# Cycling a group's experts in descending order, and moving an early expert block's products, weighing and transposes among the routing products of a one-core decoder step

## The chip, the cores and the metric

The kernel runs on one core of a Trainium2 chip. The metric is the device time in microseconds (us) of one execution; less is better. Three runs of the kernel before took 1231.51, 1237.66 and 1239.29 us.

## What is computed

One layer of a decoder: stick-breaking attention beside a convolution module, an output projection, and then a mixture of experts (MoE) over 1,056 tokens (1,024 of a prompt, 32 of samples). The change touches only the MoE and its routing. Cut to that:

```
logits = tokens @ w_router                         # 16 experts in 4 groups of 4
probs  = softmax(logits); sel = probs + b_router
best   = group with the largest sum of its two largest sel
idx    = the 2 experts with the largest sel in that group
w      = probs[idx] / sum(probs[idx])
y      = sum over the 2 experts of  w * (silu(t @ w_gate[e]) * (t @ w_up[e])) @ w_down[e]
x_out  = x + gate * y
```

Everything is float32. `w_gate[e]` and `w_up[e]` are 1024 x 512, `w_down[e]` is 512 x 1024: 2 MB each, 6 MB an expert. On the inputs that setup_inputs draws, the reference's router sends this many of the 2,112 (token, expert) pairs to experts 0 to 15: 43, 57, 52, 90 | 104, 184, 147, 39 | 116, 69, 65, 48 | 348, 115, 175, 460. Of the first 512 tokens, expert 15 has 224, more than any other.

## The kernel before, in words

**The early expert.** While the output projection and the router still run over the last token tiles, the expert with most of the first 512 tokens (here 15) is chosen, its three weights are loaded into side 0 of the weight buffers, and up to 256 of its tokens are worked on in NEB = 2 blocks of 128 rows, s = 0 and 1. A block's work is: TensorE transposes its rows (`early_turn`), `early_gate_or_up(s, 0, ...)` is the gate product and `early_gate_or_up(s, 1, ...)` the up product over k = 0 to 7 (KD = 8; one k is one 128x128 by 128x512 float32 product, two records of the trace); ScalarE takes the sigmoid, VectorE multiplies (`early_swish`, L2603) and then weighs with the up product and the router weight (`early_weigh`, L2607); TensorE transposes the result (`early_turn_act`, L1895), ScalarE copies it out of PSUM (`evac_acte`, L1335), and TensorE multiplies by w_down (`early_down(s, w)`, two halves w). VectorE ends a block with `early_combine` (L2613), and GpSimd scatters it.

**The routing.** TensorE transposes the normed rows of tile t (`route`, L1831), multiplies them with the router's weights (`router_strips`, L1842) and adds the strips (`router_sum`, L1849). With the last `router_sum` VectorE starts a long chain of small operations: the choice of experts, the mask `r_maskb` (L2693), then a wait for `rank_ready`, which TensorE gives after the rank products (L1964 to L1968), then slots, units and the ordering (L2706 to L2792). At L2790 it releases TensorE's first `to_slots` (L1978), which gives the token rows of the first passes; VectorE turns them into indices (L2797 to L2800) and GpSimd fetches those rows of x (`fetch_x`, L971). VectorE goes on with `tile_w` (L2809), the expert lists (`experts_of`, L2761 to L2777), the two `early_combine`, the copies to `w_slot` and `turned_hi(0)` (L2834). The gate product of pass 0 (L2007) waits for `turned_hi(0)`, the two combines and its weights. All of TensorE's and VectorE's order is written out by hand; each engine runs its instructions in program order.

**Units and passes.** An expert's remaining tokens are cut into units of UR = 64 rows. Units stand in one list, expert after expert. Pass t works on two units at once, unit t on side 0 and unit r_cut + t on side 1, with r_cut = max(half the units, the units of the largest group); each side has one buffer for each of the three weights. The expert order starts at the early expert, takes its group first and the other groups in a cycle, and inside each group cycles from the early expert's member number on. `expert_order` (L2585 on) computes it from `e_parts`: part 0 is each expert's group, part 1 its number in the group.

**The loop.** `step(t)` on TensorE: up product of pass t, the transposes of pass t + 1 in its middle (L1998), gate product of pass t + 1 with the transposes of the activations (L2014), down product of pass t (L2021). On SP, `refill(t)` loads w_up of pass t + 1 when the up product of pass t is done, w_gate of pass t + 2 when the gate product of t + 1 is done, and w_down of pass t + 1 when the down product of t is done, all by L782. A load is conditional: it moves nothing when the side keeps its expert. SP first waits, before the weights of pass 0 (L779 to L792), for all four gate and up products of the early blocks. GpSimd gathers x rows, residual rows and gate rows and scatters the result each pass.

Of the kernel before, what the change touches and what calls it, by code (L numbers as in the profile page):

```python
# [8 lines left out]
ALU = mybir.AluOpType  # L9
# [29 lines left out]
def decoder_step(nc, x_prompt, x_sample, cache_k, cache_v, state_conv, page_table, c_prompt, c_sample,  # L39
# [12 lines left out]
    CW, CC = conv_w.shape[1:]  # L52
    TAIL = CW - 1
    E, _, F = w_gate.shape[1:]
    EG = 4
    EPG = E // EG
    KD = D // P
# [44 lines left out]
    with ctx:  # L102
        def sb(name, shape, dt=F32):
            return ctx.enter_context(nc.sbuf_tensor(name, shape, dt))
# [68 lines left out]
        e_parts_i = sb("e_parts_i", [P, 2, E], I32)  # L173
        e_parts = sb("e_parts", [P, 2, E])
# [124 lines left out]
        def early(*shape, dt=F32):  # L299
# [10 lines left out]
            if len(shape) == 3:  # L310
# [81 lines left out]
                   "lgT_ps": ("c_sig", 1), "lgT_sb": ("rows_done", 2), "w_in_read": ("pool_const", 2),  # L392
                   "own_staged": ("ada_used", 32)}
        S |= {n: S[m] for n, (m, _) in (routing | merging).items()}

        MM_ALL = NCHUNK * NTP + 1
# [652 lines left out]
        def _(act):  # L1049
# [281 lines left out]
            def early_sigmoid(s):  # L1331
                act.wait_ge(S["e_gu"], N0["e_gu"] + s + 1)
                nc.scalar.activation(acte[:, s, :], bank[:, EG_BANK[s], :], ACT.Sigmoid).then_inc(S["e_sig"], 1)

            def evac_acte(s):  # L1335
                act.wait_ge(S["e_aps"], N0["e_aps"] + s + 1)
                nc.scalar.activation(acteT[:, s, :, :], bank[:, EA_BANK[s], :].rearrange("p (k n) -> p k n", k=KF), ACT.Copy)\
                    .then_inc(S["e_asb"], 1)
# [39 lines left out]
            nc.scalar.activation(r_e, r_z, ACT.Exp).then_inc(S["exp_ready"], 1)  # L1378
            for s in range(NEB):
                early_sigmoid(s)  # L1380
            act.wait_ge(S["hot_ready"], N0["hot_ready"] + 1)
            nc.scalar.activation(at_row32, at_row, ACT.Copy).then_inc(S["row32_ready"], 1)
            evac_acte(0)
            act.wait_ge(S["eq_ready"], 1)
            nc.scalar.activation(tile_id[:, :, 0, :], tile_id[:, :, 2, :], ACT.Copy, scale=part[:, 0:1])\
                .then_inc(S["part_ready"], 1)
# [44 lines left out]
        def _(pe):  # L1431
# [394 lines left out]
            def route(t):  # L1826
                pe.wait_ge(S["h2_done"], N0["h2_done"] + t + 1)
                if t >= 1:
                    pe.wait_ge(S["h2T_sb"], 2 * t)
                for k in range(KD if t < NTP else 2):  # L1830
                    mm = pe.transpose(bank[:, 4 + k // 4, (k % 4) * P:(k % 4 + 1) * P], h2[t % 2][:, k * P:(k + 1) * P],  # L1831
                                      identf[:, :])
                mm.then_inc(S["h2_ps"], 1)

            def router_strips(t):
                pe.wait_ge(S["h2T_sb"], 2 * t + 2)
                for i in range(KD // 4):
                    for j in range(4):
                        k = KD // 4 * j + i
                        n, turned = (P, h2T[:, t % 2, k, :]) if t < NTP else \  # L1840
                            (NS, h2T[:, t % 2, k % 2, NS * (k // 2):NS * (k // 2 + 1)])
                        mm = pe.matmul(lg_strip[NS * j:NS * j + E, t % 2, 0:n], wr[:, k, :], turned,  # L1842
                                       start=(i == 0), stop=(i == KD // 4 - 1))
                mm.then_inc(S["lgT_ps"], 1)

            def router_sum(t):
                n = P if t < NTP else NS
                pe.wait_ge(S["lgT_sb"], N0["lgT_sb"] + t + 1)
                pe.matmul(bank[0:n, 6, t * E:(t + 1) * E], lgT[:, t % 2, 0:n], strip_sum[:, 0:E], start=True, stop=True)\  # L1849
                    .then_inc(S["lg_mm"], 1)  # L1850
# [31 lines left out]
            def early_gate_or_up(s, w, k0, k1):  # L1882
                if w == 0 and k0 == 0:
                    pe.wait_ge(S["e_xsb"], N0["e_xsb"] + 2 * s + 2)
                if w == 1 and s == 1 and k0 == 0:
                    pe.wait_ge(S["h2T_sb"], 2 * NT)
                if k0 == 0:
                    pe.wait_ge(e_w_in[w], E_W0 + 16)
                for k in range(k0, k1):
                    mm = pe.matmul(bank[:, (EG_BANK, EU_BANK)[w][s], :], xeT[:, s, k, :], (wg_sb, wu_sb)[w][:, 0, k, :],  # L1890
                                   start=(k == 0), stop=(k == KD - 1))
                if k1 == KD:
                    mm.then_inc(S["e_gu"], 1)

            def early_turn_act(s):  # L1895
                pe.wait_ge(S["e_act"], N0["e_act"] + NEB + s + 1)
                for k in range(KF):
                    mm = pe.transpose(bank[:, EA_BANK[s], k * P:(k + 1) * P], acte[:, s, k * P:(k + 1) * P], identf[:, :])
                mm.then_inc(S["e_aps"], 1)

            def early_down(s, w):
                pe.wait_ge(S["e_asb"], N0["e_asb"] + s + 1)
                pe.wait_ge(e_w_in[2], E_W0 + 16)
                for k in range(KF):
                    mm = pe.matmul(bank[:, EY_BANK[s] + w, :], acteT[:, s, k, :], wd_sb[:, 0, k, w * 512:(w + 1) * 512],
                                   start=(k == 0), stop=(k == KF - 1))
                mm.then_inc(S["e_y"], 1)
# [42 lines left out]
            route(NTP - 1)  # L1950
            router_sum(NTP - 2)
            early_gate_or_up(0, 0, KD // 2, KD)
            route(NTP)
            router_strips(NTP - 1)
            early_gate_or_up(1, 0, 0, 2)
            router_sum(NTP - 1)
            router_strips(NTP)
            early_gate_or_up(1, 0, 2, 4)
            router_sum(NTP)
            early_gate_or_up(1, 0, 4, KD)  # L1960
            early_gate_or_up(0, 1, 0, KD // 2)
            pe.wait_ge(S["mask_ready"], N0["mask_ready"] + 2)
            ranks = bank[:, 0, 0:(NT + 1) * E]
            pe.matmul(ranks, identb[:, :], shift_used.rearrange("p t e -> p (t e)"), start=True, stop=False)  # L1964
# [9 lines left out]
            def to_slots(out, rows, cols, split):  # L1974
                for a in range(2 * NT):
                    n = cols(a).shape[-1]
                    for half, c0, c1 in ((slice(0, UR), 0, split), (slice(UR, P), split, n)):
                        mm = pe.matmul(out[half, :, 0:c1 - c0], rows[:, a, :], cols(a)[:, :, c0:c1],  # L1978
                                       start=(a == 0), stop=(a == 2 * NT - 1))
                mm.then_inc(S["slots_done"], 1)  # L1980

            early_gate_or_up(0, 1, KD // 2, KD)
            early_gate_or_up(1, 1, 0, 6)
            pe.wait_ge(S["hot_ready"], N0["hot_ready"] + 1)
            to_slots(bank[:, 1, 0:2 * NG].rearrange("p (w n) -> p w n", w=2), at_row,
                     lambda a: first_id[:, a, 0:2, :], NG)
            early_turn_act(0)
            early_gate_or_up(1, 1, 6, KD)
            early_down(0, 0)
            early_turn_act(1)  # L1990
            early_down(0, 1)
            pe.wait_ge(S["tok_ready"], 1)
# [123 lines left out]
        def _(dve):  # L2116
            c = Chain(dve, S["dve_c"])
            V = nc.vector
# [309 lines left out]
            c.put(V.tensor_scalar(e_parts_i[:, 0, :], row_no_i[:, 0:E], EPG.bit_length() - 1, None, ALU.arith_shift_right))  # L2428
            c.put(V.tensor_scalar(e_parts_i[:, 1, :], row_no_i[:, 0:E], EPG - 1, None, ALU.bitwise_and))
            c.wait()  # L2430
            c.put(V.tensor_copy(e_parts[:, :, :], e_parts_i[:, :, :]))
            c.put(V.tensor_copy(part[:, :], part_i[:, :]))
            c.put(V.memset(r_maskb, 0.0))
            c.put(V.memset(off_row[:, :], 0.0))
# [168 lines left out]
            def early_swish(s):  # L2603
                dve.wait_ge(S["e_sig"], N0["e_sig"] + s + 1)
                V.tensor_tensor(acte[:, s, :], acte[:, s, :], bank[:, EG_BANK[s], :], ALU.mult).then_inc(S["e_act"], 1)

            def early_weigh(s):  # L2607
                dve.wait_ge(S["e_gu"], N0["e_gu"] + NEB + s + 1)
                dve.wait_ge(S["e_act"], N0["e_act"] + NEB)
                V.scalar_tensor_tensor(acte[:, s, :], bank[:, EU_BANK[s], :], ew_slot[:, s:s + 1], acte[:, s, :],  # L2610
                                       ALU.mult, ALU.mult).then_inc(S["e_act"], 1)
# [86 lines left out]
                               AX_X, ALU.add))  # L2698
            for j in range(NEB):
                early_swish(j)  # L2700
            dve.wait_ge(S["rank_ready"], N0["rank_ready"] + 1)

            total = bank[:, 0, NT * E:(NT + 1) * E]
# [76 lines left out]
            def by_token(cols, n):  # L2780

                return cols.unsqueeze(1).broadcast_to([P, 2 * NT, n]), r_unit.unsqueeze(2).broadcast_to([P, 2 * NT, n])
# [7 lines left out]
                               ALU.is_equal))  # L2790
            dve.sem_inc(S["hot_ready"], 1)
            V.tensor_tensor(tile_id[:, :, 2, :], *by_token(unit_no, NC), ALU.is_equal).then_inc(S["eq_ready"], 1)  # L2792
            early_weigh(0)

            dve.wait_ge(S["slots_done"], N0["slots_done"] + 1)
            first = bank[:, 1, 0:2 * NG].rearrange("p (w n) -> p w n", w=2)
# [11 lines left out]
            dve.wait_ge(h2_stored[1], 16 * 4)  # L2808
            op(V.tensor_tensor(tile_w, tile_id[:, :, 2, :], r_w.unsqueeze(2).broadcast_to([P, 2 * NT, NC]), ALU.mult))  # L2809
            dve.sem_inc(S["hot_ready"], 1)  # L2810
            early_weigh(1)
            c.put(V.tensor_scalar(r_gm, units, -1.0, None, ALU.add))
            c.put(V.tensor_scalar(r_half, r_cut, -1.0, None, ALU.add))
            c.wait()
# [148 lines left out]
```

## Time and profile before

| | us |
|---|---|
| three runs | 1231.51, 1237.66, 1239.29; median 1237.66 |
| the profiled execution, its own time | 1229.6 |
| its span (first to last instruction) | 1227.9 |
| TensorE busy | 1152.1 |
| VectorE busy | 618.8 |
| mean granted TensorE clock | 0.987 of full |

Times of the trace are counted from the start of the span. The routing lies at about 740 to 790 us, the 18 passes of the MoE at 790 to 1220 us.

### The profile page before, as it was taken

Reading aid. Unit: us, or ns where it says so; the run is one execution under the profiler, and the core shown is the slowest. Engines: PE = TensorE matmul, PEld = TensorE weight load, DVE = VectorE, ACT = ScalarE, POOL = GpSimd, SP = SyncE. Lnnn points to the kernel's source line nnn. Section 1 sums busy time; section 2 is a strip of 40 time slices with the busy share of each in tenths; the row PEclk is TensorE's granted clock in tenths of the full one; section 3 lists DMA queues with packets and bytes.
Section 4 is the critical chain, followed back from the end, with each engine's and each line's share of the span. In section 5 each row is a group of like instructions: output and inputs, shape, how many; then the busy total and the mean of one; then the engine's idle time right before and its main releaser. Section 6 shows DMA issues by size and latency. Waiting matters only on the chain.

```text
span 1227.9 us, 19158 instructions
## 1 busy us (share of the span) xinstructions
PE 1152.1 (94%) x6692; PEld 541.4 (44%) x6692; DVE 618.8 (50%) x1254; ACT 341.2 (28%) x719; POOL 248.1 (20%) x303
## 2 busy tenths in 40 slices
PE   6999999999989889998999998989999999889995
PEld 4444444444436566665544453433333333333332
DVE  0010867786779999997974476611112121112112
ACT  2132221222137888887312321100000000000000
POOL 2011101221049600000010010112223222222222
PEclk9999999999999999999999999999999999999998
DMA  9943333322347454645332273779984668988983
GB/s 358 335 145 103 103 103 108 94 91 86 90 153 256 147 192 163 230 141 189 139 109 97 86 261 126 270 287 331 348 310 168 231 214 322 377 306 300 333 324 138
DMA packets 114100, 250.76 MB, mean 204 GB/s; under 512 B 14446, under 2 KB 28910, under 8 KB 113000
## 3 DMA queue, kind: packets, MB, share of 16 engines
q1 hardware_dynamic: 93345, 206.85, 48.0%
q0 software_dynamic: 16704, 38.30, 8.8%
q10 hardware_dynamic: 3984, 4.72, 1.1%
q8 instruction: 42, 0.69, 0.2%
q14 instruction: 25, 0.20, 0.1%
HBM read 370.93 MB, written 38.17 MB: 333 GB/s over the span
## 4 chain that ended last, share of the span: by engine, by line
PE 72%; DMA 10%; DVE 6%; issue 5%; ACT 4%; SPq 1%; POOL 0%; ACTq 0%; POOLq 0%; DVEq 0%
PE bank L1598 20%; PE bank L2007 15%; PE bank L2021 7%; PE bank L1789 6%; DMA low<-out_dram,o_col 3%; PE bank L1578 3%; PE bank L1632 2%; PE bank L1672 2%; DMA out_dram<-mid,o_col 2%; PE bank L1682 2%; DMA big<-in_w_up_dram 2%; PE bank L1660 2%; PE bank L1453 1%; ACT mid L1231 1%; PE bank L1695 1%
## 5 line engine op out<-in xcount | busy, mean ns | idle before, releaser
L2007 PE MATMUL bank<-big,mid 128*64 128x512 f32 x1120 | 255.0, 602 | 13.0 <-DMA big<-in_w_gate_dram 7.2
L1598 PE MATMUL bank<-big 128*128 128x512 f32 x560 | 249.2, 598 | 0.1
L1598 PEld LDWEIGHTS bank<-big 128*128 128x128 f32 x560 | 103.6, 190 | 131.3 <-issue 131.3
L2182 DVE SCALAR_TENSOR_TENSOR cvT<-low,cw,cvT 128x256 f32<-128x256 f32 x360 | 156.9, 514 | 0.0
L2007 PEld LDWEIGHTS bank<-big,mid 128*64 128x64 f32 x1120 | 79.4, 138 | 161.0 <-issue 160.2
L2021 PE MATMUL bank<-big,mid 128*64 128x512 f32 x544 | 119.6, 592 | 0.0
L2287 DVE TENSOR_TENSOR_SCAN big<-big 128x513 f32<-128x513 f32 (+4 forms) x96 | 90.3, 980 | 8.4 <-ACT big L1198 8.4
L2897 DVE TENSOR_TENSOR mid<-bank,low 128x512 f32<-128x512 f32 x34 | 21.9, 686 | 126.8 <-DMA low<-out_dram,o_col 81.0
L2878 DVE TENSOR_TENSOR xt<-xt,bank 128x512 f32<-128x512 f32 x18 | 12.4, 687 | 140.4 <-ACT xt L1395 140.4
L889 POOL TENSOR_TENSOR st<-st,mhalf 128x16 f32<-128x16 f32 (+1 forms) x9 | 25.2, 2801 | 254.3 <-DVE st L2213 245.5
L2021 PEld LDWEIGHTS bank<-big,mid 128*64 128x64 f32 x544 | 39.1, 137 | 77.7 <-issue 77.7
L1390 ACT ACTIVATE mid<-bank 128x512 f32<-128x512 f32 x18 | 10.8, 598 | 190.2 <-PE bank L1998 190.2
L1789 PE MATMUL bank<-mid,cvT 128*128 128x512 f32 x128 | 58.2, 602 | 1.1 <-DVE cvT L2390 1.1
L1789 PE MATMUL bank<-mid,big 128*128 128x512 f32 x128 | 58.1, 596 | 0.0
L1198 ACT ACTIVATE big<-bank,nbb 128x512 f32<-128x512 f32 (+3 forms) x96 | 50.9, 586 | 17.3 <-PE bank L1638 11.9
L1660 PE MATMUL bank<-identf,big 128*128 128x128 f32 x288 | 45.8, 286 | 9.4 <-ACT big L1221 3.3
L2297 DVE TENSOR_TENSOR big<-big 128x512 f32<-128x512 f32 (+3 forms) x96 | 53.3, 592 | 0.4
L1211 ACT ACTIVATE big<-bank,bb 128x512 f32<-128x512 f32 (+3 forms) x96 | 51.3, 601 | 0.0
L1003 POOL DMA_INDIRECT out_dram<-mid,o_col x17 | 17.1, 1004 | 167.5 <-DVE mid L2899 167.5
L2338 DVE SCALAR_TENSOR_TENSOR cvT<-low,cw,cvT 128x256 f32<-128x256 f32 x120 | 50.8, 489 | 0.0
L1083 ACT ACTIVATE big<-bank,low 128x128 f32<-128x128 f32 x64 | 23.4, 468 | 90.7 <-PE bank L1492 58.5
L1632 PE MATMUL bank<-big 64*128 64x512 f32 (+3 forms) x192 | 44.9, 545 | 3.2 <-ACT big L1211 2.0
(460 smaller groups left out, 1386.9 us busy)
## 6 DMA issues: line engine op xcount, KB each, us to landing
big<-in_w_gate_dram SPq DMA_DIRECT2D x39, 2048.0 KB, 9.3
big<-in_w_up_dram SPq DMA_DIRECT2D x37, 2048.0 KB, 8.3
big<-in_w_down_dram SPq DMA_DIRECT2D x37, 2048.0 KB, 13.6
low<-in_w_ada_dram SPq DMA_DIRECT2D x32, 512.0 KB, 4.1
low<-in_cache_v_dram SPq DMA_DIRECT2D x64, 256.0 KB
big<-in_w_in_dram SPq DMA_DIRECT2D x8, 1280.0 KB, 17.1
xt<-in_x_prompt_dram SPq DMA_DIRECT2D x16, 512.0 KB, 4.7
mid<-in_w_ada_dram SPq DMA_DIRECT2D x8, 1024.0 KB, 14.0
```

The source lines that it names most:

```text
L1198: nc.scalar.activation(keep[w][h][:, first:first + n], bank[:, 2 * (i % 2) + h, 0:n], ACT.Sigmoid, scale=-(HD ** -0.5), bias=nbb[:, 2 * pa ...
L1211: nc.scalar.activation(sig[w][h][:, b0 * P:b1 * P], bank[:, 2 * (i % 2) + h, 0:n], ACT.Sigmoid, scale=HD ** -0.5, bias=bb[:, 2 * pair + h: ...
L1598: mm = pe.matmul(bank[:, 4 if cc == 2 else cc, :], hT[:, s, k, :], w_in_sb[:, k, cc * 512:(cc + 1) * 512], start=(k == 0), stop=(k == KD - 1))
L1632: mm = pe.matmul(bank[:, 2 * (i % 2) + h, 0:n], stage[64 * h:64 * h + 64, s, 0, qb * P:(qb + 1) * P], stage[64 * h:64 * h + 64, s, 1, b0 * ...
L1660: mm = pe.transpose(bank[:, TURN_BANK["a", 2 * i + h], (kb - b0) * P:(kb - b0 + 1) * P], sig[u % 2][h][:, kb * P:(kb + 1) * P], identf[:, :])
L1789: mm = pe.matmul(bank[:, 2 * (t % 2) + cc, :], cat[:, k % NPAIR, t * P:(t + 1) * P], w_out_sb[:, k, cc * 512:(cc + 1) * 512], start=(k == ...
L2007: mm = pe.matmul(bank[half, 2 * s + w, :], xgT[:, s, k, half], w_sb[:, x, k, :], start=(k == 0), stop=(k == KD - 1))
L2021: mm = pe.matmul(bank[half, 6 + w, :], actT[:, s, k, half], wd_sb[:, x, k, w * 512:(w + 1) * 512], start=(k == 0), stop=(k == KF - 1))
L2182: c.put(V.scalar_tensor_tensor(out, src, cw[:, ch, tap:tap + 1], out, ALU.mult, ALU.add))
L2287: V.tensor_tensor_scan(kept, kept, kept, 1.0, ALU.mult, ALU.bypass).then_inc(S["scan_done"], 1)
L2297: V.tensor_tensor(sig[w][h][:, b0 * P:b1 * P], sig[w][h][:, b0 * P:b1 * P], keep[w][h][:, first + b0 * P:first + b1 * P], ALU.mult).then_i ...
L2338: c.put(V.scalar_tensor_tensor(out, x, cw[:, ch, tap:tap + 1], out, ALU.mult, ALU.add))
```

## The change

It does three things: (a) part 1 of `e_parts` becomes 3 minus the member number, so that inside each group the cycle runs downwards (15, 14, 13, 12 and not 15, 12, 13, 14), with one more small VectorE operation for it; (b) on TensorE, pieces of the early blocks' products move among the routing products, and the first transpose of the activations and a down product move ahead of the first `to_slots`; (c) on ScalarE and VectorE, `evac_acte(0)` and both `early_weigh` move to earlier places.

```diff
@@ ScalarE
             for s in range(NEB):
                 early_sigmoid(s)
+            evac_acte(0)
             act.wait_ge(S["hot_ready"], N0["hot_ready"] + 1)
             nc.scalar.activation(at_row32, at_row, ACT.Copy).then_inc(S["row32_ready"], 1)
-            evac_acte(0)
@@ TensorE
             early_gate_or_up(0, 0, KD // 2, KD)
+            early_gate_or_up(1, 0, 0, 3)
             route(NTP)
             router_strips(NTP - 1)
-            early_gate_or_up(1, 0, 0, 2)
+            early_gate_or_up(1, 0, 3, 4)
             router_sum(NTP - 1)
             router_strips(NTP)
-            early_gate_or_up(1, 0, 2, 4)
+            early_gate_or_up(1, 0, 4, 5)
             router_sum(NTP)
-            early_gate_or_up(1, 0, 4, KD)
-            early_gate_or_up(0, 1, 0, KD // 2)
+            early_gate_or_up(1, 0, 5, KD)
+            early_gate_or_up(0, 1, 0, KD)
             pe.wait_ge(S["mask_ready"], N0["mask_ready"] + 2)
@@ TensorE
-            early_gate_or_up(0, 1, KD // 2, KD)
             early_gate_or_up(1, 1, 0, 6)
+            early_turn_act(0)
+            early_gate_or_up(1, 1, 6, KD)
+            early_down(0, 0)
             pe.wait_ge(S["hot_ready"], N0["hot_ready"] + 1)
             to_slots(bank[:, 1, 0:2 * NG].rearrange("p (w n) -> p w n", w=2), at_row,
                      lambda a: first_id[:, a, 0:2, :], NG)
-            early_turn_act(0)
-            early_gate_or_up(1, 1, 6, KD)
-            early_down(0, 0)
             early_turn_act(1)
@@ VectorE
-            c.put(V.tensor_copy(e_parts[:, :, :], e_parts_i[:, :, :]))
+            c.put(V.tensor_copy(e_parts[:, 0, :], e_parts_i[:, 0, :]))
+            c.put(V.tensor_scalar(e_parts[:, 1, :], e_parts_i[:, 1, :], -1.0, EPG - 1.0, ALU.mult, ALU.add))
@@ VectorE
             for j in range(NEB):
                 early_swish(j)
+            early_weigh(0)
             dve.wait_ge(S["rank_ready"], N0["rank_ready"] + 1)
@@ VectorE
             V.tensor_tensor(tile_id[:, :, 2, :], *by_token(unit_no, NC), ALU.is_equal).then_inc(S["eq_ready"], 1)
-            early_weigh(0)
+            early_weigh(1)
 
             dve.wait_ge(S["slots_done"], N0["slots_done"] + 1)
@@ VectorE
             dve.sem_inc(S["hot_ready"], 1)
-            early_weigh(1)
```

## Rows read from the trace of the kernel before

**Rows 1.** The page's chain that ended last, by engine.

```profile
PE 72%; DMA 10%; DVE 6%; issue 5%; ACT 4%; SPq 1%; POOL 0%; ACTq 0%; POOLq 0%; DVEq 0%
```

**Rows 2.** Timeline of PE, 736 to 801 us: start, us, engine, line, shapes, [idle before].

```profile
736.44 3.68 PE L1890 MATMUL bank<-big 128*128 128x512 f32 x8
742.18 0.44 PE L1831 MATMUL bank<-identf,low 128*128 128x128 f32 x2 [2.06 <-DVE low L2476]
...
747.30 0.24 PE L1849 MATMUL bank<-strip_sum,big 128*32 128x16 f32 x2
...
756.30 0.24 PE L1964 MATMUL bank<-big,identb 128*128 128x160 bf16 x1 [1.70 <-DVE r_maskb L2693]
...
765.59 0.73 PE L1978 MATMUL bank<-first_id,low 128*64 128x4 bf16 x36
767.71 0.69 PE L1898 MATMUL bank<-identf,xt 128*128 128x128 f32 x4 [1.38 <-DVE xt L2610]
768.20 3.58 PE L1890 MATMUL bank<-big 128*128 128x512 f32 x4
...
786.75 2.94 PE L1978 MATMUL bank<-low 128*64 128x40 f32 x108
790.33 10.52 PE L2007 MATMUL bank<-big,mid 128*64 128x512 f32 x48 [0.64 <-issue]
```

**Rows 3.** Timeline of DVE, 757 to 791 us.

```profile
757.14 1.29 DVE L2605 TENSOR_TENSOR xt<-xt,bank 128x512 f32<-128x512 f32 x2
758.34 0.43 DVE L2706 TENSOR_TENSOR mid<-bank,ramp 128x272 f32<-128x272 f32 x1
...
766.90 0.75 DVE L2610 SCALAR_TENSOR_TENSOR xt<-bank,ew_slot,xt 128x512 f32<-128x512 f32 x1
767.57 0.15 DVE L2797 COPY mid<-bank 128x2 f32<-128x2 f32 x1
...
772.48 0.14 DVE L2812 TENSOR_SCALAR mid<-mid 128x1 f32<-128x1 f32 x1
...
782.14 1.29 DVE L2619 TENSOR_TENSOR cvT<-bank,low 128x512 f32<-128x512 f32 x2 [0.26 <-DVE pass_exp L2777]
...
789.54 0.69 DVE L2834 COPY mid<-bank 128x512 f32<-128x512 f32 x1
```

**Rows 4.** Timeline of PE in the loop, 809 to 1111 us.

```profile
809.30 5.26 PE L2007 MATMUL bank<-big,mid 128*64 128x512 f32 x16 [3.84 <-DMA big<-in_w_gate_dram]
...
879.94 3.65 PE L2007 MATMUL bank<-big,mid 128*64 128x512 f32 x16 [1.28 <-DVE mid L2834]
...
1055.93 1.09 PE L1998 MATMUL bank<-identf,mid 128*128 128x128 f32 x8
1063.98 5.35 PE L2007 MATMUL bank<-big,mid 128*64 128x512 f32 x16 [3.37 <-DMA big<-in_w_gate_dram]
...
1084.26 3.65 PE L2007 MATMUL bank<-big,mid 128*64 128x512 f32 x16 [3.89 <-DMA big<-in_w_up_dram]
1087.85 1.09 PE L1998 MATMUL bank<-identf,mid 128*128 128x128 f32 x8
...
1110.36 1.10 PE L1998 MATMUL bank<-identf,mid 128*128 128x128 f32 x8
```

**Rows 5.** Timeline of SP: when the weight loads of L782 were issued (two sides each).

```profile
797.83 0.83 SPq L782 DMA_DIRECT2D big<-in_w_gate_dram  x2
...
1046.11 1.10 SPq L782 DMA_DIRECT2D big<-in_w_gate_dram  x2
...
1061.21 4.50 SPq L782 DMA_DIRECT2D big<-in_w_up_dram  x2
```

**Rows 6.** Windows: length, busy us of PE, PEld, DVE, ACT, POOL; PEclk, DMA share, GB/s.

```profile
809.30:815.00 5.70, 5.70 (x20) 1.96 (x20) 0.00 (x0) 0.00 (x0) 0.00 (x0) 0.71 1.03 396
...
1061.00:1084.30 23.30, 16.43 (x70) 5.61 (x71) 3.85 (x5) 1.19 (x2) 4.72 (x7) 0.93 1.02 383
```

**Rows 7.** DMA issues after 800 us, median us from issue to landing.

```profile
mid<-h_d,x_col POOLq DMA_INDIRECT x18, 7.7
```

## The prediction

> **What bounds the kernel now.** I read the chain that ended last first: TensorE holds 72% of it and DMA 10% [rows 1], so a change pays where TensorE stands idle or at half clock. Next came TensorE's timeline over the two stretches that the change touches. In the routing it idles 2.06 us before the last `route`, 1.70 before the rank products and 1.38 before the transpose of block 0, and the four records after that take 3.58 us where eight took 3.68 before [rows 2]: two k at the lower of its two clock levels, some 1.7 us lost. After that it is busy to pass 0, which starts at 790.33, just after VectorE's `turned_hi(0)` of 789.54 + 0.69 [rows 2, 3]. In the loop the trace shows a pass each 22.51 us (1087.85 to 1110.36) except where weights come late: the gate product of pass 1 waits 3.84 us, a `turned_hi` behind a late gather holds that of pass 4 for 1.28 us, and from pass 11 to pass 12 the transposes stand 31.92 us apart, 9.41 over the usual 22.51 [rows 4]. That is 3.37 for w_gate, 3.89 for w_up and half clock after the first: 5.35 us for sixteen records that take 3.65 otherwise.
>
> **Part 1, the order.** Expert 15 keeps 460 - 224 = 236 pairs, 4 units. With units of 64 the experts 0 to 15 have 1, 1, 1, 2 | 2, 3, 3, 1 | 2, 2, 2, 1 | 6, 2, 3, 4 units, 36 in all; the largest group has 15, so r_cut = 18 and there are 18 passes, in both kernels. Before, side 0 runs 15 (4 units), 12 (6), 13 (2), 14 (3), 3 (2), 0 (1), and side 1 runs 1, 2, 7 (1 each), 4 (2), 5 (3), 6 (3), 11 (1), 8, 9, 10 (2 each). A new expert is due at passes 4, 10, 12, 15, 17 on side 0 and 1, 2, 3, 5, 8, 11, 12, 14, 16 on side 1. The only pass with both is 12, and it follows 10 and 11: just where the 9.41 us are [rows 4]. After, side 0 is 15 (4), 14 (3), 13 (2), 12 (6), 3 (2), 2 (1), due at 4, 7, 9, 15, 17; side 1 is 1, 0, 7 (1 each), 6 (3), 5 (3), 4 (2), 11 (1), 10, 9, 8 (2 each), due at 1, 2, 3, 6, 9, 11, 12, 14, 16. Fourteen loads of 6 MB both times. Again one pass has both, now 9, but pass 8 has none, nor has 10.
>
> So the double is not removed; it gets an empty queue. Its w_gate was issued at 1046.11, w_up at 1061.21 [rows 5], and at full share DMA moves 396 GB/s, 383 over the whole stretch with w_up [rows 6]; I take 0.40 MB a us. A double weight is 4.19 MB. The gathers and the scatter are four of 0.52 MB a pass. Let G be the issue of the double w_gate of pass 9. Its product was due at G + 14.5 before (1063.98 - 3.37 = 1060.61 against 1046.11). The w_gate load of pass 1, issued at 797.83 and in at 809.2, took 11.4 us for 2.1 MB and about three gathers, 3.67 / 0.40 = 9.2 us, so I put 2 us ahead of the first byte. With these and 4.19 / 0.40 = 10.5 us it lands at G + 12.5; the x gather of the pass has gone before it, since with light DMA the chain of gathers runs ahead. No wait. (If 1 MB of gathers falls in, G + 15: 0.5 us.) The double w_up is issued at G + 15.1 and starts at G + 17; with three gathers beside it, 5.75 MB / 0.40 = 14.4 us, it lands at G + 31.3. It is due after gate and down products, 14.5 us behind G + 14.5 or G + 29.1. Wait: 2.2 us. The double w_down has 16 us and 6.3 MB: just in time. Before, w_up had the rest of w_gate and w_down of pass 11 ahead, hence its wait and the full share of 1.02. So the double costs 2.1 us rather than 9.41: **-7.3 us**. Bounds: nothing (-9.4) and both waits kept at some two thirds of their size with one half-clock stretch (-3). Passes 1 to 4 load as before and keep the 1.28; pass 5 is now free, worth 0.2 us that I set against the extra `e_parts` operation, on a VectorE with slack.
>
> **Part 2, the routing stage.** One k costs 3.68 / 8 x 2 = 0.92 us with its tail, 0.88 by the pitch [rows 2].
> - Three k fill the idle before the last `route`: they end at 740.0 + 2.65 = 742.65, so `route` starts 0.47 late, but two k fewer (-1.76) stand between it and the last `router_sum`, which moves from 747.30 to 746.0: VectorE's whole choice of experts runs 1.3 us earlier, the mask is ready at 755.0.
> - TensorE then has 3 + 8 k = 9.7 us, to 755.95, so ranks start there (before 756.30) without idling, and are out at 756.6. VectorE's swishes end 1.3 earlier, about 757.1; `early_weigh(0)` adds 0.67 in front of L2706, which starts at 757.75 and not 758.34. Ranks hide behind the weighing. Gain on VectorE's chain 0.6 us.
> - TensorE: six k, the transpose (0.5), two k, a down product (3.45) end at 767.5. The first `to_slots` is released at 764.9 and now waits behind these: 767.5 to 768.2, where it ran at 765.59. What is queued behind that on others: L2797 (767.57) starts at 768.35, 0.8 later, and with it the x fetch. VectorE loses the 0.8 but no longer stops 1.3 us for the second weighing, so L2812 comes at 771.3 for 772.48, `early_combine(0)` at 780.9 for 782.14.
> - TensorE, without gaps and without the 1.7 us of half clock, ends the last down product at 779.05. The second combine used to wait for it; now it follows the first directly, 780.9 + 2 x 2.56 = 786.0. Then `w_slot` 0.44 and `turned_hi` 0.69: pass 0 can start at 787.3 for 790.33. **-3.0 us.** VectorE is the bound now; TensorE has finished its 1.0 of transposes and 2.94 of slots by 783.0 and idles 4.3 us.
>
> That idle has a price. Idle stretches of 3.84 and 3.37 us were followed by 5.26 and 5.35 us for sixteen records, that of 3.89 by 3.65 [rows 4], the granted clock after the first being 0.71 [rows 6]. So between 0 and 1.7 us are lost in the gate product of pass 0; two of three, and the one behind slot products with few columns, say yes: **+1.65**. The Trainium skill, TensorE: Matmul & The Clock Gate, the section on HAM oscillation, says that waits between bursts of products put the clock back to its lower level so that each burst begins slow. By that rule the loss is full here; the row of 3.89 shows that it isn't certain.
>
> **Part 3, what follows at pass 1.** SP waits for the four early products; the last ends at 764.05, before 771.8. So the 6 MB of pass 0 start 7 us earlier and are through by 782, and DMA is empty when the blocks are scattered; the gathers of pass 0 start some 3 us earlier against the gate load of pass 1. That load was issued at 797.83 and arrived 11 us later, DMA at full share [rows 5, 6]; its product is due 8.06 us after issue plus 0.4. If gathers of 0.5 to 1 MB have left before, it comes 1.3 to 2.6 us sooner, and half clock in pass 0 stretches nothing else. I take 0.9 us left of 3.84, **-2.9 us**, and with so short a stop no half clock after it (the 1.28 us stop had none [rows 4]), **-1.6 us**. Bounds: wait and clock loss kept (0), both gone (-5.5).
>
> Sum: -7.3 - 3.0 + 1.65 - 2.9 - 1.6 = -13.1 us. The profiled execution of 1229.6 would be 1216.5. It lies 8.1 us under the median of the runs; I subtract the same from the median: 1237.7 - 13.1 = 1224.6 us.
>
> **Rivals.**
> - A: the x fetch is late. It is issued 0.8 us later and now comes after, not before, the 6.3 MB of weights. Its landing was 7.7 us in the median [rows 7], for it to matter it must need over 12.8 (TensorE needs it by 782). If it waited for the weights, 766.6 + 16 = 782.6, and its own 1.05 MB gives 785.2, then 1.0 + 2.94 + 1.1: pass 0 at 790.3, nothing gained there. Only -7.3 and perhaps -1: 1230 us. For: DMA share 1.03 in such stretches. Against: gathers in the loop land in 7.7 beside weights. The Trainium skill, DMA: Bandwidth & Descriptors, section on queues, rings and completion order, says that each DMA engine takes turns among the queues that have work, a packet at a time; by that rule the fetch gets its share and this rival falls.
> - B: the double keeps its price, because what made it dear is its 12.6 MB alone and not what stood ahead. Then only parts 2 and 3 remain, -5.8: 1232 us. For: three double weights in a row still use all of DMA. Against: the fluid sum above. The same time comes out if the direction did not move the double at all.
> - C, slower: at pass 9 all three double weights are late, not two, each by what the rows show (3.84, 3.37, 3.89) with half clock after each (1.65): 16.1 us for 9.41, so +6.7, and the start's gain of 5.8 doesn't cover it: +0.9, 1238.6 us. It decides when w_down's 6.3 MB take over 16 us, below 0.39 MB a us; 383 GB/s over a stretch is under that, but a late w_up also moves w_down's due time, which speaks against it.
>
> **How the numbers follow.** The forecast 0.54, A 0.19, B 0.20, C 0.07. A measurement of this kernel can tell about 1% (12.4 us) from nothing. The forecast's own spread (bounds of part 1 -9.4 to -3, of parts 2 and 3 -9 to -1) puts it beyond 1% in nearly nine tenths, as timed runs sit above the profiled one and so seem to wait more than it: 0.48. The rest and A and B are within 1% but for few: 0.46. C past 1% or trouble unseen: 0.06. Range: -20 to -1 around 1237.7, 1217 to 1236.
>
> **What would show it.** Right: no 31.9 us pass at pass 12; the passes around 9 together 2 us long, waiting for w_up; the last `router_sum` at 746.0; L2706 at 757.75; first slots at 767.5; pass 0 at 787.3 behind `turned_hi`, with about 4 us idle before it and a clock under 1; the wait for pass 1's w_gate near 1 us. Wrong: a wait for the x rows before L1998 at 779, waits for weights at pass 9 summing to over 6 us, or VectorE standing before `early_weigh(0)`.

## The result, and the profile after

Ten runs of the changed kernel have a median of 1226.86 us (1224.46 to 1230.49), ten of the kernel before beside them 1238.01 us (1231.51 to 1244.97): a ratio of 0.9919 with a 95% interval of 0.9896 to 0.9942, 0.8% faster. The forecast was 1224.6 us with a range of 1217 to 1236. The profiled execution of the changed kernel took 1228.0 us, only 1.6 us less than that of the kernel before (1229.6): the first is near its median, the second lies under all ten runs of its kernel. So the two traces are compared stretch by stretch here, and what a stretch costs in general is read from the fourteen traces of this study.

The page of the changed kernel, span and chain, against [rows 1]:

```profile
span 1226.2 us, 19159 instructions
...
PE 76%; DMA 8%; DVE 6%; ACT 5%; issue 4%; SPq 0%; ACTq 0%; POOL 0%; POOLq 0%; DVEq 0%
```

DMA gave up 2 points of the chain, and TensorE's share is 4 points up. TensorE's timeline of the changed kernel over the routing, against [rows 2]:

```profile
738.94 6.25 PE L1890 MATMUL bank<-big 128*128 128x512 f32 x14
745.03 0.38 PE L1831 MATMUL bank<-identf,low 128*128 128x128 f32 x2
...
748.38 0.24 PE L1849 MATMUL bank<-strip_sum,big 128*32 128x16 f32 x2
...
758.09 0.23 PE L1965 MATMUL bank<-big,identb 128*128 128x160 bf16 x1
...
769.53 0.73 PE L1979 MATMUL bank<-first_id,low 128*64 128x4 bf16 x36
...
781.96 2.94 PE L1979 MATMUL bank<-low 128*64 128x40 f32 x108
789.23 13.19 PE L2007 MATMUL bank<-big,mid 128*64 128x512 f32 x48 [4.33 <-DVE mid L2835]
```

From the last common product to 784.90, the end of the slot products, TensorE runs without a gap now; the three idle stretches of 2.06, 1.70 and 1.38 us are gone. In their place stands one of 4.33 us before pass 0, and it waits for VectorE. The 48 records behind it take 13.19 us where they took 10.52. VectorE, against [rows 3]:

```profile
759.63 0.75 DVE L2611 SCALAR_TENSOR_TENSOR xt<-bank,ew_slot,xt 128x512 f32<-128x512 f32 x1
760.30 0.43 DVE L2708 TENSOR_TENSOR mid<-bank,ramp 128x272 f32<-128x272 f32 x1
...
770.31 0.16 DVE L2799 COPY mid<-bank 128x2 f32<-128x2 f32 x1 [0.70 <-PE bank L1979]
...
783.07 1.29 DVE L2620 TENSOR_TENSOR cvT<-bank,low 128x512 f32<-128x512 f32 x2 [0.26 <-DVE pass_exp L2779]
784.40 1.23 DVE L2622 TENSOR_TENSOR cvT<-cvT,low 128x1024 f32<-128x1024 f32 x1
785.54 1.28 DVE L2620 TENSOR_TENSOR cvT<-bank,low 128x512 f32<-128x512 f32 x2
...
788.43 0.69 DVE L2835 COPY mid<-bank 128x512 f32<-128x512 f32 x1
```

The second combine follows the first with no gap, and `turned_hi(0)` ends at 789.12, 0.1 us before pass 0. The clock there, in windows of the changed kernel (columns as in [rows 6]):

```profile
789.00:796.00 7.00, 6.78 (x20) 2.41 (x22) 2.73 (x18) 0.00 (x0) 2.55 (x4) 0.60 0.32 127
796.00:802.00 6.00, 6.00 (x30) 2.02 (x26) 0.69 (x1) 0.60 (x1) 2.71 (x4) 1.00 0.60 174
```

The loop, against [rows 4]:

```profile
812.42 4.97 PE L2007 MATMUL bank<-big,mid 128*64 128x512 f32 x16 [5.39 <-DMA big<-in_w_gate_dram]
...
989.48 1.09 PE L1998 MATMUL bank<-identf,mid 128*128 128x128 f32 x8
997.23 3.65 PE L2007 MATMUL bank<-big,mid 128*64 128x512 f32 x16 [3.07 <-DMA big<-in_w_gate_dram]
...
1014.16 3.65 PE L2007 MATMUL bank<-big,mid 128*64 128x512 f32 x16 [2.24 <-DMA big<-in_w_up_dram]
1017.75 1.09 PE L1998 MATMUL bank<-identf,mid 128*128 128x128 f32 x8
```

Pass 12 is like any other; the double stands at pass 9 and costs 28.27 - 22.51 = 5.76 us over, for 9.41. But pass 1 waits 5.39 us for w_gate where it waited 3.84.

Where the first pair of traces hides the gain: TensorE's first long group of projection products.

```profile
22.34 15.69 PE L1578 MATMUL bank<-big 128*128 128x512 f32 x36 [2.16 <-ACT big L1083]
```

That was the kernel before; the changed one:

```profile
23.23 17.38 PE L1578 MATMUL bank<-big 128*128 128x512 f32 x36 [2.16 <-ACT big L1083]
```

No edit lies there, yet by the last common product before the routing the changed kernel's trace is 2.5 us late (738.94 for 736.44). At an L1731 product ahead of every edit the traces of this study stand between 573.6 and 577.9 us, 574.8 before and 577.3 after. Whether that is scatter between executions isn't shown: the second traces of the same two kernels stand at 574.6 and 577.5, each within 0.2 us of its first, so it may as well belong to the program as built. It is left out of the sums below, but a difference of a few us between two medians may come from there.

### The profile page after: what moved, and what is told of

Same layout as the page of the kernel before. It is cut to its first block, busy times and chain, and to the rows that moved or that the text cites. A ratio compares the mean times of both kernels' runs of the same rounds, so it can differ in the third digit from the quotient of the medians.

```text
span 1226.2 us, 19159 instructions
## 1 busy us (share of the span) xinstructions
PE 1152.6 (94%) x6692; PEld 541.3 (44%) x6692; DVE 619.2 (50%) x1255; ACT 340.8 (28%) x719; POOL 248.1 (20%) x303
## 4 chain that ended last, share of the span: by engine, by line
PE 76%; DMA 8%; DVE 6%; ACT 5%; issue 4%; SPq 0%; ACTq 0%; POOL 0%; POOLq 0%; DVEq 0%
PE bank L1598 20%; PE bank L2007 16%; PE bank L2021 7%; PE bank L1789 7%; PE bank L1578 3%; DMA low<-out_dram,o_col 3%; PE bank L1632 2%; PE bank L1890 2%; PE bank L1672 2%; PE bank L1682 2%; PE bank L1660 2%; DMA out_dram<-mid,o_col 2%; DMA big<-in_w_up_dram 2%; PE bank L1453 1%; ACT mid L1231 1%
```

## The experiments

Each kernel was timed beside the kernel before, and has one trace. The runs came in three groups, e1 to e4, e5 to e8 and e9 to e12, in which the kernel before had medians of 1236.26, 1239.52 and 1238.30 us; across groups the ratio to it is the better measure. "After" below is the changed kernel.

**The order alone (e1).** The kernel before with only the `e_parts` edit.

```diff
-            c.put(V.tensor_copy(e_parts[:, :, :], e_parts_i[:, :, :]))
+            c.put(V.tensor_copy(e_parts[:, 0, :], e_parts_i[:, 0, :]))
+            c.put(V.tensor_scalar(e_parts[:, 1, :], e_parts_i[:, 1, :], -1.0, EPG - 1.0, ALU.mult, ALU.add))
```

> Only the descending cycle, everything else as before. Theory 1 (the order makes most of the gain, by giving the double load of pass 9 an empty queue): 6 to 10 us under the kernel before in the median; in the trace the pass with both loads costs 5.8 us over 22.51 and stands at pass 9, not 9.4 at pass 12. Rival (the gain is from the routing stage): under 3 us in the median.

1227.05 us for 1236.26, ratio 0.9916 (0.9884 to 0.9948): nearly all of the gain. Its trace was taken in the slowest of its nine executions (1232.46 us). In it the passes 2 to 8 lie exactly 22.51 us apart and pass 9 costs 4.64 over, but pass 1 costs 9.20:

```profile
1001.94 5.10 PE L2007 MATMUL bank<-big,mid 128*64 128x512 f32 x16 [2.57 <-DMA big<-in_w_gate_dram]
1018.26 3.65 PE L2007 MATMUL bank<-big,mid 128*64 128x512 f32 x16 [0.19 <-DMA big<-in_w_up_dram]
```

All passes together are 13.9 us over, for 17.0 and 20.2 in the two traces of before, so the loop of this trace shows 3 to 6 of the 9.2 us. In the routing it even loses time: the last `router_sum` stands 12.58 us behind the last common product, for 10.86, since the idle of 2.20 us before the last `route` was followed by half clock (3.09 us for four records that take 1.98 otherwise). In e9, with the same old places, it was so again; in the two traces of before it wasn't.

**The places alone (e2).** After with the old `e_parts` line (the diff above reversed).

> Only the moved products, weighing and transposes, the order ascending as before. Theory 1: 1 to 4 us under the kernel before; pass 0 starts 3.5 us earlier against the last early product before the routing, but its sixteen first records run at half clock and the wait for w_gate of pass 1 stays at 4 to 5.5 us, so that little is left. Rival (the stage's 3.6 us are all kept and the double at pass 12 costs less, too): 5 us or more.

1234.73 us for 1236.26, ratio 0.9985 (0.9957 to 1.0014): nothing that can be told from no change. Pass 0 starts 40.81 us after the last `router_sum`, for 43.03 before, behind 4.31 us of idle; its 48 records take 12.01 us, and w_gate of pass 1 is waited for 7.18 us.

**Both again (e3, e4).** The two kernels unchanged, for second traces.

> The kernel before, unchanged, for a second trace. Its profiled execution was 8 us under the median of its runs. Theory 1 (typical executions wait longer for weights in the loop than the profiled one did): a trace near the median shows over 9.4 us at pass 12 and more than 1.7 us in the passes 3 to 5. Rival (the difference lies ahead of the routing, as the 2.5 us between the two traces at 736 us do): the loop as in the first trace and the last product before the routing later.

> The changed kernel, unchanged, for a second trace on this chip. Theory 1: 11 us under the kernel before in the median; idle of about 4.3 us before pass 0, a wait of 4 to 5.5 us for w_gate of pass 1, 5 to 6 us over at pass 9. Rival (the 5.39 us wait for w_gate of pass 1 was chance): 1 to 3 us there.

Before: 1235.72 us; pass 1 costs 8.75 over (5.67 in the first trace), pass 12 10.90. So its first profiled execution was a lucky one in the loop, by 3.2 us over all passes. The passes 3 to 5 cost 0.37 only, which my theory had above 1.7. After: 1225.72 us, ratio 0.9909 (0.9877 to 0.9940); idle 4.30, wait at pass 1 5.57, pass 9 3.90, under the 5 to 6 expected. The wait of 5.39 was no chance. Against e2, in the same group of runs, the order is worth 9.0 us by the medians, as it was alone (9.2).

**No pass with two loads (e5).** After, but only the early expert's group descends: `e_parts` is as before the change, and on `b_two`, after the wrap, a member part x over 0 becomes 4 - x where the group part is 0.

```diff
+                c.put(V.tensor_scalar(b_wrap[:, 0, :], b_two[:, 0, :], 0.0, None, ALU.is_le))
+                c.put(V.tensor_scalar(b_wrap[:, 1, :], b_two[:, 1, :], 0.0, None, ALU.is_gt))
...
+                op(V.tensor_tensor(b_two[:, 1, :], b_two[:, 1, :], b_wrap[:, 0, :], ALU.add))
```

> The changed kernel, but only the early expert's own group cycles downwards, the others upwards as before: side 0 takes a new expert at passes 4, 7, 9, 15, 17, side 1 at 1, 2, 3, 5, 8, 11, 12, 14, 16, so no pass has both. Theory 1 (what costs is a pass with both loads, by the queue): the 4 to 6 us over at pass 9 fall under 1, the median 3 to 5 us under the changed kernel. Rival (the loads at 7, 8 and 9 in a row cost the same): no change, waits over 3 us at passes 8 and 9.

1224.80 us, ratio 0.9885 (0.9853 to 0.9917), against 0.9919 and 0.9909 for after: the intervals overlap, and the 3 to 5 us that theory 1 has are not clear of noise. The passes 8 and 9 cost nothing now, as theory 1 says. But the ascending side 1 brings a load at pass 5 back, the fifth in a row, and there the trace has what I had priced at 0.2 us:

```profile
906.71 5.35 PE L2007 MATMUL bank<-big,mid 128*64 128x512 f32 x16 [3.50 <-issue]
```

3.50 us of waiting and half clock after it, 5.42 over for that pass, 0.42 for the one ahead. The wait is put down to nothing in this row, but VectorE shows its end:

```profile
903.27 1.29 DVE L2904 TENSOR_TENSOR mid<-bank,low 128x512 f32<-128x512 f32 x2 [13.60 <-DMA low<-out_dram,o_col]
...
905.73 0.68 DVE L2841 COPY mid<-bank 128x512 f32<-128x512 f32 x1
```

The combine stood waiting for its residual rows, `turned_hi` comes behind it in VectorE's order and ended at 906.41, and the product started 0.3 us later. So this pass was held by a late gather and not by a late weight.

**The gathers held back (e6).** After, with one wait on GpSimd.

```diff
+            pool.wait_ge(wg_in[1], 32)
             gather_out(0, 0, 1, 16)
```

> The changed kernel; GpSimd starts the gathers of output rows of pass 0 only when w_gate of pass 1 has landed. Theory 1 (the wait for w_gate of pass 1 comes from gathers that run beside it): it lands some 8 us after issue rather than 13, the wait falls from 5.5 to about 0 to 1 us, 4 to 7 us less in the median with the half clock gone. Rival (2 MB takes that long by itself at this place): the wait stays over 4 us and the median within 2 us.

1227.21 us, nothing won in the median, yet both halves of it are instructive:

```profile
808.16 3.65 PE L2008 MATMUL bank<-big,mid 128*64 128x512 f32 x16 [1.97 <-DMA big<-in_w_gate_dram]
...
882.31 4.97 PE L2008 MATMUL bank<-big,mid 128*64 128x512 f32 x16 [5.79 <-DVE mid L2836]
```

The wait at pass 1 falls to 1.97 us and the half clock behind it goes: the product starts 9.6 us after the issue of w_gate, not 13.0. The gathers held it up. Then the gathers themselves are late, and at pass 4 TensorE waits 5.79 us for a `turned_hi` that stands on VectorE behind a combine whose rows are late: 7.32 over for that pass. The gain was given back three passes later.

**The combines ahead of the long list (e7).** After, on VectorE.

```diff
-            experts_of(MT, pass_exp)
-            dve.sem_inc(S["tiles_ready"], 1)
             for j in range(NEB):
                 early_combine(j)
...
             turned_hi(0)
+            experts_of(MT, pass_exp)
+            dve.sem_inc(S["tiles_ready"], 1)
```

> The changed kernel; VectorE's long expert list for all passes comes after the two combines and turned_hi(0), not before. Theory 1 (VectorE's chain alone sets the start of pass 0): it starts 3 to 3.5 us earlier, TensorE idles about 1 us before it and keeps the full clock; 3 to 5 us less if the wait for w_gate of pass 1 doesn't grow. Rival (that wait takes it back, since the gathers and the load meet anyway): the start is earlier, the median within 1.5 us.

1218.00 us, ratio 0.9842 (0.9810 to 0.9875), 9 us under after, where theory 1 had 3 to 5. VectorE:

```profile
779.33 1.29 DVE L2620 TENSOR_TENSOR cvT<-bank,low 128x512 f32<-128x512 f32 x2
...
782.39 1.29 DVE L2620 TENSOR_TENSOR cvT<-bank,low 128x512 f32<-128x512 f32 x2 [0.51 <-PE bank L1905]
...
785.94 0.69 DVE L2833 COPY mid<-bank 128x512 f32<-128x512 f32 x1
```

and TensorE:

```profile
786.73 10.52 PE L2007 MATMUL bank<-big,mid 128*64 128x512 f32 x48 [0.64 <-issue]
...
804.90 3.65 PE L2007 MATMUL bank<-big,mid 128*64 128x512 f32 x16 [3.04 <-DMA big<-in_w_gate_dram]
```

VectorE waits for TensorE again. The span is 1215.2 us for 1226.2. Pass 0 starts 37.15 us after the last `router_sum` (which ran at 749.58), 3.7 earlier than in after, at full clock. The wait at pass 1 fell, too, to 3.04, for a reason that I had not put in the expectation. SP issued the load at 794.23, and GpSimd, which now gets its indices later, its gathers behind it (the next fence); in after those of L990 to L998 stood ahead of a load issued at 799.39, and only the x gathers behind (the one after that). The double at pass 9 fell as well, from 5.76 to 2.67 us; why isn't shown.

```profile
795.58 1.06 POOL L990 DMA_INDIRECT low<-out_dram,o_col  x1 [0.92 <-POOL o_col L984]
796.94 0.96 POOL L992 DMA_INDIRECT low<-g_d,o_col  x1 [0.30 <-issue]
803.40 1.00 POOL L998 DMA_INDIRECT low<-out_dram,o_col  x1 [5.50 <-DMA low<-out_dram,o_col]
```

```profile
795.56 0.96 POOL L992 DMA_INDIRECT low<-g_d,o_col  x1 [0.30 <-issue]
798.12 1.00 POOL L998 DMA_INDIRECT low<-out_dram,o_col  x1 [1.60 <-DMA low<-out_dram,o_col]
...
800.11 0.98 POOL L979 DMA_INDIRECT mid<-h_d,x_col  x1 [0.79 <-POOL x_col L976]
```

**Filler in the idle (e8).** After, with four products whose result nothing reads.

```diff
+            pe.wait_ge(S["e_done"], N0["e_done"] + 1)
+            for k in range(4):
+                pe.matmul(bank[:, 6, :], identf[:, :], cv_flat[:, 0:512], start=True, stop=True)
```

> The changed kernel with four products of 128x512 that nothing reads put into the idle before pass 0, 3.5 us of work. Theory 1 (the idle sets the clock back and that costs 1.5 to 2.7 us in pass 0): the first 48 records of the loop take 10.5 us rather than 12.2 to 13.2, the clock is full there, and the median falls by 1 to 2.5 us. Rival (the wait for w_gate of pass 1 swallows it, as its load is issued at the end of the gate product, or the clock falls for another reason): median within 1 us.

1226.51 us, no change; the rival holds, and the trace shows both sides:

```profile
784.42 3.70 PE L2040 MATMUL bank<-cvT,identf 128*128 128x512 f32 x8 [0.77 <-DVE cvT L2625]
788.05 10.52 PE L2007 MATMUL bank<-big,mid 128*64 128x512 f32 x48
...
810.47 6.08 PE L2007 MATMUL bank<-big,mid 128*64 128x512 f32 x16 [7.28 <-DMA big<-in_w_gate_dram]
```

The idle did set the clock back: filled, the 48 records take 10.52 us. But the wait for w_gate grows from 5.4 to 7.28. Counted from the last `router_sum`, its load goes out 2.6 us sooner, and it takes 14.8 us for 12.9.

**Combines first in three other settings (e9, e10, e11).** The e7 edit on e1, on e5, and on e2.

> Descending order and the combines ahead of the long expert list, but the products, weighing and transposes in their old places. Theory 1 (the moved products shorten TensorE's side, which the old place of the list hid): the second combine still waits for the last early down product at 785.9 of the first trace, so pass 0 starts within 1 us of before and the median lies within 2 us of the order alone (1227). Rival (the place of the list is worth 3 to 4 us by itself): 1222 to 1224.

1227.74 us, ratio 0.9904 (0.9873 to 0.9936): theory 1. Without the moved products pass 0 starts 43.02 us after the last `router_sum`, as before; the place of the list is worth nothing there, since the second combine waits for TensorE, 4.26 us here.

> The kernel with the combines first, with the mixed order that has no pass with two loads but five passes in a row with one and then three more. Theory 1 (a row of five loads without a pause loses what the double loses, through late gathers or weights): 0 to 5 us over near pass 4 or 5 instead of the 2.7 at pass 9, the median within 2 us of 1218. Rival (the loss there was chance): 2.5 to 4 us under it.

1214.55 us, ratio 0.9809 (0.9781 to 0.9836), the fastest kernel of the study and 3.5 us under e7 by the median: the number of the rival. The traces don't show it in the loop. All passes together are 5.70 us over here and 5.99 in e7, as 2.67 us saved at pass 9 stand against half clock at pass 1, where e7 had none, and 0.57 at pass 5. But this trace stands at 573.6 us at the L1731 product ahead of every edit and e7's at 577.9, and that is 4.3 of the 4.8 us between their spans. What the missing double is worth stays open. The row of five cost little this time, again behind VectorE's combine:

```profile
800.65 5.35 PE L2007 MATMUL bank<-big,mid 128*64 128x512 f32 x16 [3.16 <-DMA big<-in_w_gate_dram]
...
892.96 3.65 PE L2007 MATMUL bank<-big,mid 128*64 128x512 f32 x16 [0.34 <-issue]
```

> All moved places and the combines first, but the ascending order. Theory 1 (the order is worth 7 to 10 us in any setting): 1225 to 1229, with 8 to 11 us over at pass 12. Rival (the double was only dear because the loop began late at pass 1): under 1222.

1228.30 us, ratio 0.9919 (0.9890 to 0.9949), 10.3 above e7, from which it differs by the order alone: theory 1. Pass 12 costs 11.75 over, and the passes 4 and 5 1.48 and 6.81. At pass 5 TensorE waits 4.89 us, as in e5 behind a combine for whose residual rows VectorE stood idle:

```profile
894.59 1.29 DVE L2897 TENSOR_TENSOR mid<-bank,low 128x512 f32<-128x512 f32 x2 [14.98 <-DMA low<-out_dram,o_col]
```

Most of such an idle costs nothing: in e1, where TensorE doesn't wait at these passes, VectorE idles 9.47 and 6.54 us for its rows.

**x rows before output rows (e12).** e7, with one gather moved ahead on GpSimd.

```diff
+            pool.wait_ge(S["xg_ps"], 1)
+            gather_x(2, 0, 1)
             for s in range(NEB):
                 pool.wait_ge(out_st[s], EARLY)
-            gather_out(0, 0, 1, 16)
-            pool.wait_ge(S["xg_ps"], 1)
-            gather_x(2, 0, 2)
+            gather_out(0, 0, 2, 16)
```

> The kernel with the combines first; GpSimd fetches the x rows of pass 2 before it waits for the scatters of the early blocks, in a stretch where DMA stands idle. Theory 1 (each 0.5 MB of gathers that runs beside w_gate of pass 1 delays it by about 1.3 us): the wait there falls from 3.0 to 1 to 2 us and the median by 1 to 2 us, without the late gather at pass 4 that holding all of them back brought. Rival (no change, since other gathers close up): within 0.5 us.

1220.82 us, ratio 0.9855 (0.9828 to 0.9883), against e7's 1218.00, so if anything slower. The stretch was not idle for long: the gather was issued at 792.47, 1.3 us behind w_gate (791.21), and the wait at pass 1 was 4.50 us, not 1 to 2. The load took 1.4 us longer with this gather beside it than in e7, near the 1.3 that theory 1 has for 0.5 MB; the theory was wrong in where the gather would fall.

**The fourteen traces side by side** (us over the 22.51 of a pass, from one L1998 group to the next; "landing" is from the issue of w_gate of pass 1 on SP to the start of its product, less 0.1; "xb" is when the gather of L998 was issued against that load):

```
                       xb    landing  pass 1  passes 3-5  the double
before                +4.8   11.4      5.67      1.69      9.41
e3 before again       +3.7   14.0      8.75      0.37     10.90
e1 order              +3.9   15.0      9.20      0         4.64
e2 places             +0.3   14.7      8.94      0        10.46
after                 -1.3   12.9      6.93      0.10      5.76
e4 after again        -0.3   13.1      8.36      0         3.90
e5 no double          -0.7   13.0      8.00      5.84      none
e8 filler             +2.1   14.8      9.93      0         7.12
e12 x before out     +11.2   12.0      6.17      0         3.50
e7 combines first     +9.2   10.6      3.27      0         2.67
e9 order, combines    +9.1   10.8      5.22      0         6.84
e10 no double, comb.  +9.3   10.7      5.09      0.57      none
e11 places, combines  +9.8   10.1      2.77      8.29     11.75
e6 gathers wait      +18      9.5      2.31      7.82      2.78
```

With the gather of L998 and the x gathers after it 9 us or more behind the load, it lands in 9.5 to 10.8 us (12.0 where one x gather was put beside it), otherwise in 11.4 to 15.0. Only e6 and e12 move gathers and nothing else. The double costs 9.4 to 11.8 in the four traces of the ascending order and 2.7 to 7.1 in the eight of the descending one. A load at pass 5 (six traces: before, e2, e3, e5, e10, e11) comes with 0 to 8.3 us in passes 3 to 5, mean 2.8; without it seven of eight show 0.1 or less, and the eighth is e6 with its late gathers. At pass 5 alone it is 0.19, 0.01, 0, 5.42, 0.57 and 6.81 us with the load, mean 2.2, and 0.01 or less in all eight without. Of what is lost at pass 4, 1.28 us in before and 1.25 in e11 are waits of its gate product, behind which that load is only issued, so they can't be its price.

## Why the prediction was right or wrong

The time, its side and the range held: 1226.9 for 1224.6, and a gain of 11.2 us for 13.1. It came about otherwise than the sum has it.

- **What bounds the kernel.** Right. The schedule of loads that I worked out from the router's counts is the one that ran: the double stands at pass 12 in all four ascending traces and at 9 in the eight descending ones.
- **Part 1, the double (-7.3 us).** The mechanism is right: the same 12.6 MB cost less behind a pass without loads. The size was off. I left 2.1 us at pass 9; the eight traces have 4.65 in the mean, for 10.6 in the four ascending, so -6.0. The step that was off is the landing of the double w_gate: I had it at G + 12.5 and no wait. It was issued at 979.66 and its product started at 997.23, G + 17.6, a wait of 3.07 us; that for w_up, 2.24, was as worked out (2.2). No run parts the pause ahead of the double from the rest of the order.
- **Part 1, "pass 5 is now free, worth 0.2 us".** Wrong in size. I had taken the price from one trace, which has 0.19 us at pass 5. Over six traces it is 2.2 in the mean and 6.8 at worst, and in both dear ones (e5, e11) it is a late gather that holds the pass. This may be a part of the gain that the sum lacked: the order alone brings 9.2 us by the medians, and its double only 6. But the two traces of before, with 0.19 and 0.01, don't show it, so what fills the 9.2 is open.
- **Part 2, the start of pass 0 (-3.0 us).** Right, step by step: last `router_sum` 9.44 us after the last common product, for 10.86, where the working gives -1.3; no idle before the ranks; `early_weigh(0)` in front of L2708, which comes 0.54 us sooner for 0.6; first `to_slots` later than before; the combines back to back; VectorE the bound with 4.33 us of idle for 4.3 worked out. From product to pass 0 it is 50.29 us for 53.89, -3.6.
- **The half clock in pass 0 (+1.65 us).** The cause is shown by e8. It was in all five traces with an idle of 4.3 us or more; the 48 records took 11.85 to 13.19 us there, so 1.3 to 2.7 more.
- **Part 3, the wait at pass 1 (-2.9 us) and its half clock (-1.6 us).** Wrong. The wait was 5.39 and 5.57 us in the two traces of after, the half clock stayed, and e2 shows the whole edit without the order to be worth 1.5 us, for the 5.8 of parts 2 and 3, and not clear of nothing. The step that failed is "if gathers of 0.5 to 1 MB have left before, it comes 1.3 to 2.6 us sooner". Counted from the last common product, the large gather of L998 went out 7.0 us earlier (59.2 us behind it for 66.2) but the load only 0.9 (60.5 for 61.4, half clock in pass 0 having taken the rest), so that the gather came from 4.8 us behind the load to 1.3 ahead of it, beside the load and not out of its way. Held back altogether (e6) the gathers free 3.4 us. That their place explains the whole wait is not shown: the two traces of before differ by 2.6 us in the landing with L998 at nearly the same place.
- **Rival A** (late x rows) didn't happen: no wait before the transposes at 780.99. **Rival B** was off in the double, which did become cheaper; its total of 1232 would have needed the start's full gain. **C** didn't happen: no w_down was waited for.
- **The base.** I subtracted 13.1 us from the median as if the traced execution and a median one waited alike. The second trace of before shows that they don't: 4.6 us more at the passes 1 and 12 together (3.08 and 1.49), 1.3 less at the passes 3 to 5. Its own execution was under its median too, so traces don't show all of what a median run loses.

So the total is in part luck: the order brought 9.2 us where the sum had 7.3, all the rest 1.5 where it had 5.8, and these errors have opposite signs. What stays open: why the landing at pass 1 varies by 2.6 us or more among traces with like gathers (11.4 and 14.0 in the two of before), why a fifth load in a row costs 0 once and 6.8 us another time, why the double got cheaper still in e7, and what moves the stretch ahead of the routing by up to 4 us.

## What to carry to other kernels

Where loads are conditional, write down which step brings which load, and look at how they are spaced, not at how many there are: here two at once cost 2.7 to 7.1 us behind a pass without loads and 9.4 to 11.8 behind two with them, and a single trace may show next to nothing of a price that is several us in others. Look, too, at what the loads delay: in e5 and e11 it was a gather of rows. A shortened stage pays when the next bound moves too: here the moved products were worth 1.5 us alone; with VectorE's list out of the way, which took two lines, they start pass 0 5.9 us earlier and take the ratio from 0.9904 (e9) to 0.9842 (e7). And before one counts on an earlier transfer, one asks what is issued beside it: holding the gathers back freed 3.4 us at an urgent load here, and cost 7.3 three passes later.

## What was unexpected in the hardware

A 2 MB load that starts with DMA otherwise nearly idle (e6) took 9.5 us from issue to use, and 11.4 to 15.0 with three gathers of 0.5 MB about it. And of idle stretches on TensorE, 4.3 us or more before pass 0 were followed by half clock in each of five traces, while 3.89 [rows 4] and 3.07 in after were not, and 1.38 behind slot products [rows 2] was. Before the gate product of the double, e4 and e6 both idle 1.97 us, and e4 has half clock behind it and e6 has not; before the last `route`, 2.20 and 2.19 us were in e1 and e9 while 2.06 and 2.15 were not in the two traces of before: the length of the idle alone doesn't tell.
